# Three column chunks of the first projection formed while the rows' quarters come in

## What is computed

```
mod = silu(c) @ w_mod[l] + b_mod[l]            # 2048 x 6144 weights, one row
shift, scale, gate = split(mod, 3)
h = rmsnorm(x, norm_gain[l]) * (1 + scale) + shift
proj = h @ w_in[l]                             # q, k, v, gates, index queries and keys
att = sparse_attention(...)                    # index scores, top 64 of 256 keys, 8 heads
ret = retention(...)                           # 8 heads, two chunks of 128 rows
x = x + gate * (concat(att * silu(g_a), groupnorm(ret) * silu(g_b)) @ w_out[l])
```

## Time and profile before

| | |
|---|---|
| median of 3 runs | 1872.98 us (1871.44 to 1873.73) |
| the profiled execution's own time | 1872.03 us, span 1869.9 us |
| PE busy | 1833.9 us, 98% |
| DVE busy | 1293.6 us, 69% |
| ACT busy | 960.3 us, 51% |
| chain that ended last | 95% PE, 2% DMA |
| DMA | 424.11 MB, mean 227 GB/s |

### The profile page before, as it was taken

How to read it: one execution, slowest core, us unless ns; L and a number is a source line. 1 busy time by engine, 2 the same in 40 slices (tenths; PEclk the granted TensorE clock), 3 DMA queues, 4 the chain that set the end, 5 groups by cost and what they waited for, 6 DMA issues and landing times.

```text
span 1869.9 us, 25534 instructions
## 1 busy us (share of the span) xinstructions
PE 1833.9 (98%) x9840; PEld 1495.0 (80%) x9840; DVE 1293.6 (69%) x1909; ACT 960.3 (51%) x1311; POOL 203.8 (11%) x261
## 2 busy tenths in 40 slices
PE   7889999999999999999999999999999999999998
PEld 4458788888888878888888888888888888888886
DVE  4239999989987778856765544488885466665555
ACT  6234455446446445544654644476765445444464
POOL 1000002100000000210000000044441020031001
PEclk9889999999999999999999999999999999999999
DMA  8999978975986986744465565554555555556552
GB/s 327 353 352 353 321 240 298 319 239 173 328 306 217 360 281 225 245 158 158 127 223 183 181 202 184 199 175 164 179 172 184 186 189 184 188 180 247 181 195 97
DMA packets 211828, 424.11 MB, mean 227 GB/s; under 512 B 7680, under 2 KB 12684, under 8 KB 210316
## 3 DMA queue, kind: packets, MB, share of 16 engines
q1 hardware_dynamic: 209788, 414.94, 65.7%
q10 hardware_dynamic: 1936, 7.76, 1.0%
HBM read 418.45 MB, written 4.21 MB: 226 GB/s over the span
## 4 chain that ended last, share of the span: by engine, by line
PE 95%; DMA 2%; DVE 1%; ACT 1%; issue 0%; SPq 0%; ACTq 0%; DVEq 0%; POOLq 0%; POOL 0%
PE acc L714 28%; PE acc L716 28%; PE acc L715 28%; DMA raw<-in_w_mod 2%; PE tps L836 1%; PE tps L755 1%; PE tps L795 1%; PE acc L875 1%; PE acc L876 1%; PE acc L877 1%; PE sps L821 0%; PE sps L942 0%; PE sps L1045 0%; PE tps L1037 0%; PE sps L1001 0%
## 5 line engine op out<-in xcount | busy, mean ns | idle before, releaser
L1892 DVE TENSOR_TENSOR w_lo<-raw,w_hi 128x1024 fp32r<-128x1024 f32 (+1 forms) x580 | 721.2, 1249 | 440.3 <-ACT w_hi L1295 438.4
L1295 ACT ACTIVATE w_hi<-raw 128x1024 fp32r<-128x1024 f32 (+1 forms) x580 | 606.4, 1051 | 761.7 <-PE acc L716 685.3
L714 PE MATMUL acc<-w_hi,ht_hi 128*128 128x512 f32 (+1 forms) x2304 | 910.5, 395 | 0.5 <-issue 0.4
L716 PE MATMUL acc<-w_hi,ht_lo 128*128 128x512 f32 (+1 forms) x2304 | 894.0, 388 | 0.0
L715 PE MATMUL acc<-w_lo,ht_hi 128*128 128x512 f32 (+1 forms) x2304 | 892.5, 387 | 0.0
L716 PEld LDWEIGHTS acc<-w_hi,ht_lo 128*128 128x128 f32 x2304 | 432.5, 188 | 90.3
L714 PEld LDWEIGHTS acc<-w_hi,ht_hi 128*128 128x128 f32 x2304 | 432.9, 188 | 87.5 <-issue 2.9
L715 PEld LDWEIGHTS acc<-w_lo,ht_hi 128*128 128x128 f32 x2304 | 433.3, 188 | 83.4
L2022 DVE SCALAR_TENSOR_TENSOR scr<-raw,vcol,scr 128x512 f32<-128x512 f32 x154 | 110.9, 762 | 4.7 <-DMA raw<-in_w_mod 0.2
L2022 DVE SCALAR_TENSOR_TENSOR proj<-raw,vcol,proj 128x512 f32<-128x512 f32 x70 | 52.3, 788 | 1.9
L2709 POOL TENSOR_TENSOR scr<-scr 128x128 f32<-128x128 f32 x56 | 31.1, 587 | 157.1 <-DVE scr L2451 157.1
(11 more groups left out here) (309 smaller groups left out, 1438.5 us busy)
## 6 DMA issues: line engine op xcount, KB each, us to landing
raw<-in_w_in SPq DMA_DIRECT2D x208, 1024.0 KB, 5.1
raw<-in_w_mod SPq DMA_DIRECT2D x64, 1024.0 KB, 5.7
raw<-in_w_mod SPq DMA_DIRECT2D x64, 512.0 KB, 7.5
raw<-in_w_out SPq DMA_DIRECT2D x32, 1024.0 KB, 5.3
raw<-in_w_o SPq DMA_DIRECT2D x16, 1024.0 KB, 5.1
...
```

The source lines that it names most:

```text
L714: pe.matmul(o, hi_m, w_hi[:, slot, u, 0:width], start=start, stop=False)
L716: mm = pe.matmul(o, lo_m, w_hi[:, slot, u, 0:width], start=False, stop=stop)
L1295: act.activation(w_hi[:, x % SPL, :, 0:width], raw[:, j, 2 * (x % halves):2 * (x % halves) + 2, 0:width], ACT.Copy).then_inc(hi_ready, 1)
L1892: dve.tensor_tensor(w_lo[:, x % SPL, :, 0:width], raw[:, j, 2 * (x % halves):2 * (x % halves) + 2, 0:width], w_hi[:, x % SPL, :, 0:width]. ...
```

## The change

In the front, three w_in slots a quarter are landed instead of two (FRONT = 3, 11 slots a quarter instead of 10) and PE does six halves, q from 0 to 5. The third chunk (chunk 2 in the order) is added up in `sps`. The six halves go round the four places of `w_hi`. The tiles of h are formed by DVE (`form`) instead of ACT, ahead of its `w_lo`. Behind the front chunk 2 falls away, so layer 0 starts with chunk 3. Its four w_mod pieces move: chunk 6 has pieces at halves 1, 3, 5, 7 instead of 1, 3, and chunk 7 at 5, 7, where it had none. Each piece is now 256 contracted rows by 1024 columns, still 1 MB, done by two DVE instructions of 1024 elements instead of four of 512; a group n has 1024 columns, eight pieces and no add of halves. The gate columns of layer 0 are turned at half 9 of chunks 6 and 7 instead of half 4, and ACT copies them at 13 instead of 8.

```diff
-PIECES = [{2: FULL, 3: FULL, 4: FULL, 5: FULL, 6: (1, 3), 8: (1, 3, 7), 9: FULL, 10: FULL, 11: (1, 3, 5),
+PIECES = [{3: FULL, 4: FULL, 5: FULL, 6: FULL, 7: (5, 7), 8: (1, 3, 7), 9: FULL, 10: FULL, 11: (1, 3, 5),
            12: (5, 7), 13: (3, 7), 15: (1, 3), 16: FULL, 17: FULL, 18: (1, 3)},
+FRONT = 3
+SLOTS = 8 + FRONT
...
                 if j < 8:
                     sp.wait_ge(mod_read, 8 * i + j + 1)
                 else:
-                    sp.wait_ge(raw_read, 8 + 4 * i + 2 * (j - 7))
+                    sp.wait_ge(raw_read, 8 + 2 * FRONT * i + 2 * (j - 7))
...
             for i in range(4):
-                for q in range(4):
+                for q in range(2 * FRONT):
+                    if i == 0 and q == 4:
+                        pe.wait_ge(bias_ready, 6)
                     quarter_half(i, q // 2, q % 2)
-                    if i < 3 and q < 3:
-                        mod_slots(i + 1, 2 * q, 4 if q == 2 else 2)
-                        if q < 2:
-                            turn_rows(4 * (i + 1) + 2 * q)
-                        else:
+                    if i < 3 and q < 5:
+                        if q == 2 or q == 3:
+                            mod_slots(i + 1, 2 * q - 3, 1)
+                            turn_rows(4 * (i + 1) + 2 * (q - 2))
+                            mod_slots(i + 1, 2 * q - 2, 1)
+                        if q == 1:
+                            mod_slots(i + 1, 0, 1)
+                        if q == 4:
+                            mod_slots(i + 1, 5, 3)
                             pair_sums()
...
-                        act.activation(w_hi[:, 2 * g + h, :, :], raw[:, t % RAW, 2 * h:2 * h + 2, :], ACT.Copy)\
-                           .then_inc(hi_ready, 1)
-                        if g == 0:
-                            formed_tiles(4 * i + 2 * h)
+                        act.activation(w_hi[:, (2 * FRONT * i + 2 * g + h) % SPL, :, :], raw[:, t % RAW, 2 * h:2 * h + 2, :],
+                                       ACT.Copy).then_inc(hi_ready, 1)
+                    if g == 0:
+                        tiles_high(4 * i)
+                        tiles_high(4 * i + 2)
...
                 for u in range(2):
-                    if q or u:
+                    src, c_col = raw[:, slot, 2 * u:2 * u + 2, :], v2("c", 2 * q + u)
+                    if q == 0 and u == 0:
+                        r = dve.tensor_scalar(to, src, c_col, None, ALU.mult)
+                    else:
                         dve.wait_ge(raw_read, own.ahead(0))
+                        r = dve.scalar_tensor_tensor(to, src, c_col, to, ALU.mult, ALU.add)
...
+            def form(k):
+
+                dve.wait_ge(xt_ready, k // 2 + 1)
+                for e in range(2):
+                    scale, bias_col = of_layer(0)(k + e)
+                    r = dve.tensor_scalar(xt(k + e), xt(k + e), scale, bias_col, ALU.mult, ALU.add)
+                r.then_inc(tiles_formed, 1)
...
             for i in range(4):
                 rows_out(i)
                 columns(i)
+                dve.wait_ge(columns_ready, i + 1)
+                form(4 * i)
+                form(4 * i + 2)
+                for g in range(FRONT):
                     for h in range(2):
+                        low_halves(i, g, h)
                         if g == 0:
                             tiles_low(4 * i + 2 * h)
```

More of the change, by code:

```diff
@@ L476, in landed_start @@
         def landed_start(t):
-            return sum(32 if j % 10 < 8 else 16 for j in range(t % RAW, t + 1, RAW))
+            return sum(32 if j % SLOTS < 8 else 16 for j in range(t % RAW, t + 1, RAW))
         def full(w):
@@ L494, in slots_of_chunks @@
         def slots_of_chunks():
-            plan, item, piece = [{}, {}], 0, 4 * 8
+            plan, item, piece = [{}, {}], 0, 8 * 4
             for l in range(DEPTH):
-                for k in range(0 if l else 2, NCH + 5):
+                for k in range(0 if l else FRONT, NCH + 5):
                     rows, mods = [], {}
@@ L584, in pieces, with land_pair @@
                     sp.dma_start(raw[:, j, 0:kts, 0:width], src(j, col, width)).then_inc(raw_landed[j], 16)
+            def land_pair(slot, src):
+                sp.wait_ge(raw_read, free.next(2))
+                sp.dma_start(raw[:, slot, :, :].rearrange("p (k a) n -> p k (a n)", a=2), src).then_inc(raw_landed[slot], 16)
             def land(slot, src, width=CH):
@@ L592, in _ @@
                     mod_pair(i, j)
-                for g in range(2):
-                    slot_free(10 * i + 8 + g)
-                    slot = (10 * i + 8 + g) % RAW
+                for g in range(FRONT):
+                    slot_free(SLOTS * i + 8 + g)
+                    slot = (SLOTS * i + 8 + g) % RAW
                     sp.dma_start(raw[:, slot, :, :], full(wi[0])(i, CHUNKS[g] * CH, CH)).then_inc(raw_landed[slot], 16)
-            free.skip(16)
+            free.skip(8 * FRONT)
             for l in range(DEPTH):
                 for k, g in enumerate(CHUNKS + [NCH] + [0, 1, 2, 3]):
-                    if l == 0 and k < 2:
+                    if l == 0 and k < FRONT:
                         continue
@@ L787, in _, with mod_sums @@
             m_ready = Seen(pe, mod_ready)
-            def mod_sums(src, parts=1):
+            def mod_sums(src):
                 pe.wait_ge(mod_taken, m_taken.next())
-                if parts == 1:
-                    pe.wait_ge(mod_ready, m_ready.next())
-                for j in range(4):
-                    for e in range(parts):
-                        mm = pe.matmul(tps[:, 1, j:j + 1], src[:, e, j * P:(j + 1) * P], ones,
-                                       start=e == 0, stop=e == parts - 1)
-                mm.then_inc(mod_summed, 1)
+                m_taken.skip(1)
+                pe.wait_ge(mod_ready, m_ready.next())
+                for e in range(2):
+                    for j in range(4):
+                        mm = pe.matmul(tps[:, 1, 4 * e + j:4 * e + j + 1], src[:, e, j * P:(j + 1) * P], ones,
+                                       start=True, stop=True)
+                mm.then_inc(mod_summed, 2)
             def spread_keys(n):
@@ L1422, in scaled_rows, with tiles_high @@
                                    scale=st[:, 22 + m:23 + m]).then_inc(xs_ready, 1)
[L1424 to L1430 removed]
+            def tiles_high(k):
+                act.wait_ge(tiles_formed, k // 2 + 1)
                 act.activation(ht_hi[:, k:k + 2, :], xt(k, 2).rearrange("p (e t) -> p e t", e=2), ACT.Copy)\
@@ L1448, in _ @@
             for i in range(4):
-                for g in range(2):
-                    t = 10 * i + 8 + g
+                for g in range(FRONT):
+                    t = SLOTS * i + 8 + g
                     for h in range(2):
@@ L1560, in norms @@
                         index_relu()
+                    if x == 13 and l == 0:
+                        gate_columns()
                     if x == 4 or x == 13:
@@ L2127, in _, with low_halves @@
             bound_ratio()
+            def form(k):
+                dve.wait_ge(xt_ready, k // 2 + 1)
+                for e in range(2):
+                    scale, bias_col = of_layer(0)(k + e)
+                    r = dve.tensor_scalar(xt(k + e), xt(k + e), scale, bias_col, ALU.mult, ALU.add)
+                r.then_inc(tiles_formed, 1)
+            def low_halves(i, g, h):
+                t = (SLOTS * i + 8 + g) % RAW
+                slot = (2 * FRONT * i + 2 * g + h) % SPL
+                dve.wait_ge(hi_ready, hi.next())
+                dve.tensor_tensor(w_lo[:, slot, :, :], raw[:, t, 2 * h:2 * h + 2, :], w_hi[:, slot, :, :].bitcast(F32),
+                                  ALU.subtract).then_inc(raw_read, 1)
+                own.skip(1)
             for i in range(4):
@@ L2159, in gains_of_second @@
                 if x == 1:
-                    mod_take(19)
+                    mod_take(9)
                     gains_of_layer(1)
```

119 lines of the change are left out of this document (56 added, 63 removed).

## The result

The change makes the kernel slower. The median goes from 1872.98 us (1871.23 to 1878.04, 8 runs) to 1878.51 us (1877.36 to 1879.68, 8 runs). The ratio is 1.0028, with a 95% interval of 1.0017 to 1.0039. The predicted 1868.5, its range and its sign are all wrong.

The account below looks back on a forecast made before the run. The front was taken to wait for weights, the rest for PE. Terms -9.1 - 0.25 + 4.7 + 0.3 = -4.35 on the profiled 1872.03 gave 1867.7, forecast as a median of 1868.5 us, range 1862.5 to 1876.

Parts of the forecast that it names:

- What bounds the kernel: Whole kernel: the front waits for weights, the rest for PE, which is busy 98% of the span.
- The formula for the next copy: Front: next copy = release of last w_in slot + 5.5 + 10.85 + read; 30.4 us high clock, 33.4 low.
- my two clocks: Front at high or low clock: chunk 3 begins at 153.7 or 162.7 us, gaining 13.6 or 4.6.
- rival (c): Front: third slot released so late that the loads stop; 1879 us with a release at 17; chance 0.12.
- The clock: Front: granted clock falls in about half the hand-overs, so the middle gain is taken, -9.1 us.
- The forming on DVE: Front: DVE forming tiles instead of ACT costs PE next to nothing; four tiles taken at 0.30 us.
- The sums: Behind the front: eight double sums at 1.75 us replace fifteen at 0.95; -0.25 us.
- Chunks 6 and 7: DVE has no pause up to half 14, so moved pieces raise PE's wait from 0.27 to 5.0; +4.7 us.
- Around chunk 8: The piece at half 15 goes on just ahead of chunk 8, where GpSimd runs; +0.3 us.
- Rival (d): Pieces in chunks 6 and 7 cost nothing because DVE catches up; 1864 us or lower; chance 0.05.
- rival (a): Front: clock stays up at every hand-over, -13.6 instead of -9.1, 1864 us; chance 0.2.
- Rival (b): Front: clock falls every time, so the gaps in the loads stay; 1873 us, no change; chance 0.2.

Follow-up runs that it names:

- e2_own: Changed kernel with the third slot's halves given memory places of their own, so ACT need not wait for halves 0 and 1; 1871.07 us, ratio 0.9986.
- e6: e2_own with half 4 of each quarter done one modulation slot later; 1870.21 us, ratio 0.9978.
- e3_form_act: Changed kernel with the tiles formed by ACT again, as before the change; 1877.37 us, ratio 1.0018.
- e12_best_act: e6 with four pieces moved from chunks 6 and 7 to chunks 8, 11 and 18, and ACT forming the tiles; 1865.67 us, ratio 0.9954.
- e10_pairs: Kernel before the change with only wide pieces and eight double sums instead of sixteen single ones; 1873.25 us, ratio 1.0003.
- e11_moved: e10_pairs with chunk 2's four pieces moved as in the change, front still two chunks; 1883.12 us, ratio 1.0047.

## Why the prediction was wrong

**What bounds the kernel** was right: the front waits for weights, the rest for PE, and the loss was read at the same two places that I had named.

**The formula for the next copy** named the right chain, and its terms were too small. **This is the first step that failed: the release of the third slot, and what follows from it.** For the release I had 12.9 us behind the copy at the high clock and 15.0 at the low one; measured were 16.2, 15.7 and 15.4. In the first quarter half 0 ran wholly at the low clock: it began at 44.97 and ACT was released at 50.55, 5.6 us for a half that I had given 4. From the release to the next copy I had 17.5 us with a fast read and 18.3 with a slow one. The reads were fast (1.06 us at 107.13), and measured were 17.9, 19.2 and 19.1 (55.61 to 73.47, 89.13 to 108.33, 123.72 to 142.81). Why the last two were some 1.6 us longer is not shown. That the loads had stood is not enough as a reason: in e2_own, where they went on, 19.7 us passed from the release at 84.05 to the copy at 103.79. Two of the sums at the low clock are also 0.1 us too high (33.4 for 33.3 and 72.3 for 72.2), which changes nothing.

The copies came 34.0, 34.9 and 34.5 us apart, 103.4 us from the first to the fourth. The middle of my two clocks had 96.2 (92.8 and 99.7), so 7.2 were lost there. From the fourth copy to chunk 3 I had 21.5 or 23.6 us, and measured were 22.0, 0.6 less than the middle. So 9.1 - 7.2 + 0.6 gives the 2.5 of the trace. e2_own shows the cause: with places of their own for the last halves the front alone gains 10.7 us.

My rival (c), "the third slot is released so late that the loads stop", is what happened in the front. Its price comes near the result partly by luck: for a release at 16.2 it gave 1876.7 us, with chunk 3 at 166.4 and +4.75 behind it, where the trace has 164.8 and +8.5. I gave it 0.12, with the argument that DVE and ACT are free by then. They are; it is PE's half 0 and half 1 that they wait for, and the sentence on the release says so itself. Both of my cases took each step at its shortest, so a release later than 15.0 had no place in them.

**The clock** was given as falling in half the hand-overs. After the change it fell at the first two and stayed up at the third (`pair_sums` 1.77, 1.87 and 1.05 us). PE was busy 3.4 of the 5.4 us ahead of the first (68.0 to 73.4), 0.9 of 4 ahead of the second (104 to 108) and 3.5 of 7 ahead of the third (136 to 143), so these rows don't tell what it hangs on. In the front of e2_own the clock fell at one hand-over and in that of e6 at none, and chunk 3 began 1.1 us earlier in e6. If half 4's later place is worth nothing in itself, a fall costs about 1 us.

**The forming on DVE** at "next to nothing" cost 1.7 us in one trace (e3_form_act), most of it in the first quarter, and nothing that could be measured once the ring was out of the way (e12_best_act).

**The sums** at -0.25: e10_pairs drifts by 0.6 from chunk 3 to layer 1, so +0.6. A double sum took 1.84 us, more than my 1.75. Small.

**Chunks 6 and 7** is the second step that failed, in its size. The mechanism was right: DVE's row is unbroken and its work becomes PE's delay. From the start of chunk 3 to half 14 PE's delay grew by 6.6 us (-2.5 to +4.1), where I had 5.35 (4.7 and 0.65 of sums). The terms can be told apart. I had priced 7.05 us of pieces; from half 5 to half 14 DVE's row grew by 7.7 us (`w_lo` of half 5 starts 3.6 us earlier than in the earlier trace rows, that of half 14 4.1 later), 7.3 of them the three pieces. Of the two credits, the 1.1 us for the sums came: `w_lo` of half 5 stands 3.6 us earlier, and the front explains only 2.5 of it. The 0.5 us for the cheaper piece at half 3 did not, and why is not shown. PE's delay does not stand in one wait of 5 us: up to half 14 it is four waits of 4.0 us together and 1.7 us of the lower clock.

**Around chunk 8** I had +0.3, and it was 1.4: PE waited 0.69 us at its first half and fell back by 0.5 more by half 4. As I read it, the piece at half 15 left DVE no lead to go into chunk 8 with.

**Sum.** The trace has -2.5 in the front and +8.5 from chunk 3 to layer 1, together 6.0. Of the 8.5, 0.6 are the sums (e10_pairs), so 7.9 are what the moved pieces cost; e11_moved has 8.8 less 0.6, or 8.2. Predicted were -9.1, -0.25 and +5.0.

Rival (d), that DVE catches up, is excluded by the same rows, rival (a) by the clock at the first two hand-overs. Rival (b), the clock falling every time, had copies 33.4 us apart, and they came 34.0 to 34.9 apart although the clock stayed up once.
